# Five conditioning rows moved behind the output evictions, and the first nine rows read their shared row from PSUM

## The reference, cut to what matters

```
# first block, feed-forward
gate, val = split(h @ w_up)            # 1024 -> 2 x 2816
gate = depthwise_conv3(gate)
x = x + g2 * ((silu(gate) * val) @ w_down)     # 2816 -> 1024

# second block, conditioning (six vectors of 1024)
mod = silu(c_2) @ ada_w_2 + ada_b_2    # ada_w_2 is 1024 x 6144
shift1, scale1, gate1, shift2, scale2, gate2 = split(mod)
```

## Time and profile before

| what | value |
|---|---|
| median of 3 runs | 1310.9 us (1310.49 to 1311.98) |
| the profiled execution | 1311.85 us, its span 1310.0 us |
| PE busy | 1259.6 us, 96% of the span |
| DVE, ACT, POOL busy | 822.5, 681.6 and 702.0 us (63, 52 and 54%) |
| mean granted clock of PE | 0.984 |
| chain of work that ended last | PE 77%, DVE 8%, POOL 4%, ACT 4%, DMA 3% |

### The profile page before, as it was taken

One profiled execution on the slowest core, in us unless ns is written; L12 is line 12 of the kernel. 1 busy time (PEld: TensorE's weight loads), 2 busy tenths in 40 slices (PEclk: granted clock), 3 DMA queues, 4 the chain that ended last, 5 costly groups with the idle time before them and its releaser, 6 DMA issues.

```text
span 1310.0 us, 21756 instructions
## 1 busy us (share of the span) xinstructions
PE 1259.6 (96%) x7760; PEld 1070.7 (82%) x7760; DVE 822.5 (63%) x1452; ACT 681.6 (52%) x1273; POOL 702.0 (54%) x582
## 2 busy tenths in 40 slices
PE   8999999999998999999999999999989999999998
PEld 1688888676787799999887788766869999998886
DVE  2577652668537988888886371686267787773113
ACT  3812545685536356666323464587365655653232
POOL 0335153268343957887766824354608666666561
PEclk9999999999998999999999989899999999999999
DMA  9417549032132743223585412110302223233221
GB/s 392 193 49 276 191 161 178 17 115 80 66 116 110 284 167 118 108 96 120 182 327 204 145 65 80 50 50 34 129 1 97 98 99 125 96 103 122 96 96 65
DMA packets 27412, 166.87 MB, mean 127 GB/s; under 512 B 2976, under 2 KB 5280, under 8 KB 8656
## 3 DMA queue, kind: packets, MB, share of 16 engines
q1 hardware_dynamic: 25328, 151.31, 32.6%
q10 hardware_dynamic: 2016, 14.68, 3.0%
HBM read 163.85 MB, written 6.32 MB: 130 GB/s over the span
## 4 chain that ended last, share of the span: by engine, by line
PE 77%; DVE 8%; POOL 4%; ACT 4%; DMA 3%; issue 3%; SPq 0%; DVEq 0%; ACTq 0%; POOLq 0%
PE bank L1641 26%; PE bank L297 21%; PE bank L357 13%; PE bank L333 5%; POOL w_lo L290 2%; DMA ada_ring<-ada_dram 2%; PE bank L1514 1%; DVE ada_ring L2418 1%; PE bank L1486 1%; PE bank L777 1%; PE bank L586 1%; DVE arena L2482 1%; DMA w_raw<-w_dram 1%; PE bank L600 1%; PE bank L572 1%
## 5 line engine op out<-in xcount | busy, mean ns | idle before, releaser
L290 POOL TENSOR_TENSOR w_lo<-w_raw,w_hi 128x512 fp32r<-128x512 f32 x168 | 258.7, 1571 | 331.4 <-ACT w_hi L281 331.4
L297 PE MATMUL bank<-h_hi,w_hi 128*128 128x512 f32 x512 | 205.5, 401 | 8.7 <-DVE h_lo L473 4.1
L1641 PE MATMUL bank<-arena_rounded,w_hi 128*128 128x256 f32 x1152 | 203.2, 278 | 0.0
L297 PE MATMUL bank<-h_lo,w_hi 128*128 128x512 f32 x512 | 202.0, 395 | 0.0
L297 PE MATMUL bank<-h_hi,w_lo 128*128 128x512 f32 x512 | 201.8, 394 | 0.0
L1357 POOL TENSOR_TENSOR w_lo<-w_raw,w_hi 128x512 fp32r<-128x512 f32 x108 | 141.1, 1308 | 102.4 <-ACT w_hi L1869 100.8
L281 ACT ACTIVATE w_hi<-w_raw 128x2048 fp32r<-128x2048 f32 x46 | 88.1, 1916 | 167.4 <-PE bank L357 60.6
L1641 PEld LDWEIGHTS bank<-arena_rounded,w_hi 128*128 128x128 f32 x1152 | 174.9, 188 | 0.0
L1641 PE MATMUL bank<-arena_rounded,w_lo 128*128 128x256 f32 x576 | 159.3, 277 | 0.0
L1641 PE MATMUL bank<-h_hi,w_hi 128*128 128x256 f32 x432 | 122.2, 283 | 1.4 <-DVE arena L2334 1.1
L297 PEld LDWEIGHTS bank<-h_hi,w_hi 128*128 128x128 f32 x512 | 97.9, 191 | 31.4 <-issue 6.7
(11 more groups left out here) (329 smaller groups left out, 2896.7 us busy)
## 6 DMA issues: line engine op xcount, KB each, us to landing
w_raw<-w_dram SPq DMA_DIRECT2D x92, 1024.0 KB, 4.8
ada_ring<-ada_dram SPq DMA_DIRECT2D x30, 1024.0 KB, 5.2
ada_ring<-ada_dram ACTq DMA_DIRECT2D x14, 1024.0 KB, 4.9
arena<-ada_dram SPq DMA_DIRECT2D x4, 1024.0 KB, 9.9
arena<-x_dram SPq DMA_DIRECT2D x2, 2048.0 KB, 11.7
bias_copies<-bias_rows SPq DMA_DIRECT2D x1, 4096.0 KB, 17.7
arena<-bias_copies SPq DMA_DIRECT2D x4, 768.0 KB, 5.8
ada_ring<-rpb_dram SPq DMA_DIRECT2D x16, 128.0 KB, 9.3
```

Of the source, the lines that this page charges most:

```text
L290: last = nc.gpsimd.tensor_tensor(w_lo[b % 2][:, part], w_raw[b % 2][:, part], w_hi[b % 2][:, part], ALU.subtract)
L297: last = nc.tensor.matmul(bank[:, :], w[:, ft, k, :], x[:, k, :], start=k == first and m == 0, stop=k == final and m == 2)
L1641: last = nc.tensor.matmul(product_at[p], w[:, k], x[:, k], start=k == 0 and m == 0, stop=k == 3 and m == 2)
```

## The change

Five edits. Rows 0 to 8 take their second operand from PSUM, as one operand that spans banks 5 and 6 (the eight PSUM tensors become three, at the same places, so that this can be written); DVE waits for PE's `row2_done` there, and for ACT's copy only before the down projection. Rows 19 to 23 leave their places behind splits 9 and 11 and stand one each behind the evictions of f = 0 to 4; the five small operations stand behind the eviction of f = 5. SP's list follows: row 19 behind block 46, 20 behind 47, 21 behind 48, 22 and 23 behind 49. `SQF` moves out of the ring, and ACT's wait for the 48 goes. In the plain blocks POOL takes two of its three extra splits (`low_turned`, 128x1024) one block later.

```diff
-        SQ1, SQ2, SQF = A(A_TMP, 3, 512), A(A_SQ, 3, 512), view(ada, 0, 3, 512)
+        SQ1, SQ2, SQF = A(A_TMP, 3, 512), A(A_SQ, 3, 512), A(A_SQ + 1536, 3, 512)
...
-        DOWN_ROWS = ((9, 10), (11, 12), (13, 14), (15, 16), (17, 18), (19, 20), (21, 22, 23))
+        TURNED_BEHIND = {B_UP + 2: 2, B_UP + 4: 0, B_UP + 5: 3}
+        DOWN_ROWS, LATE_ROWS = ((9, 10), (11, 12), (13, 14), (15, 16), (17, 18)), range(19, 24)
...
             for b in range(B_DOWN + 4, B_QKV + 1):
-                if b < B_DOWN + 10:
+                if b < B_DOWN + 8:
                     load_rows(*DOWN_ROWS[b - B_DOWN - 3])
                 load_block(sp, b)
+                if b >= B_DOWN + 8 and LATE_ROWS[0] + b - B_DOWN - 8 < 24:
+                    load_rows(LATE_ROWS[0] + b - B_DOWN - 8)
+            load_rows(*LATE_ROWS[4:])
             load_block(sp, 50)
...
                 low(pool, b)
-                if b < B_UP + 5:
-                    low_turned(up1, (2, 0, 3)[b - B_UP - 2])
+                if b in TURNED_BEHIND:
+                    low_turned(up1, TURNED_BEHIND[b])
...
-                if f == 0:
-                    act.wait_ge(ada_used, 48)
...
-            dve.wait_ge(row2_out, 2)
+            dve.wait_ge(row2_done, 1)
             row = 0
             for u in range(PLAIN1 - 1):
                 plain_taps(u)
                 for k in range(2 if u else 1):
-                    add_ada2(row)
+                    add_ada2(row, row2_banks)
...
             hidden_low(9, slice(12, 14), 0)
-            rows_behind(5)
             hidden_low(10, slice(16, 18), 2)
             hidden_low(11, slice(14, 16), 0)
-            rows_behind(6)
-            dve.wait_ge(ada_used, 48)
...
             for f in range(DC):
                 dve.wait_ge(half_used, used_after(B_DOWN + 6) + f + 1)
                 nc.vector.scalar_tensor_tensor(out=XR[:, f, :], in0=ps[f][:, :], scalar=modb[:, 24 + f:25 + f], in1=XR[:, f, :],
                                                op0=ALU.mult, op1=ALU.add).then_inc(down_free, 1)
+                if f < len(LATE_ROWS):
+                    add_ada2(LATE_ROWS[f], row2)
+                if f == len(LATE_ROWS):
+                    conditioning()
                 if f < DC - 1:
                     add_squares(dve, 3, f, SQ2)
```

More of the change, by code:

```diff
@@ L128, in sem @@
             return es.enter_context(nc.semaphore(name))
-        ps = [es.enter_context(nc.psum_tensor(f"bank{i}", [P, 512], F32)) for i in range(8)]
+        banks = [es.enter_context(nc.psum_tensor(name, [P, 512 * n], F32)) for name, n in (("bank0to4", 5), ("bank56", 2), ("bank7", 1))]
+        ps = [banks[0][:, 512 * k:512 * k + 512] for k in range(5)] + [banks[1][:, 0:512], banks[1][:, 512:1024], banks[2][:, :]]
+        row2_banks = banks[1][:, :]
         w_raw = [sb(f"w_raw{s}", [P, BLK]) for s in range(2)]
@@ L2420, in add_ada1, with add_ada2 @@
                 last.then_inc(ada_used, 1)
[L2422 to L2428, removed]
-                dve.wait_ge(ada_in[j % 2], 16 * ((24 + j) // 2 - 3))
-                half_dot(j, 0)
-                half_dot(j, 1).then_inc(ada_used, 1)
+            def add_ada2(j, row):
+                dve.wait_ge(ada_in[j % 2], 16 * ((24 + j) // 2 - 3))
+                for f in range(2):
+                    at, src = 2 * j + f, ada[:, j % 2 * BLK + f * D:j % 2 * BLK + (f + 1) * D]
+                    last = nc.vector.tensor_tensor_reduce(out=src, in0=src, in1=row, scale=1.0, scalar=par_("adab2")[:, at:at + 1],
+                                                          op0=ALU.mult, op1=ALU.add, accum_out=mod2[:, at:at + 1])
+                last.then_inc(ada_used, 1)
             def outer_taps(buf, src, w, m, n, done):
@@ L2647, in rows_behind @@
                 for j in DOWN_ROWS[k]:
-                    add_ada2(j)
+                    add_ada2(j, row2)
+            dve.wait_ge(row2_out, 2)
             hidden_low(3, slice(18, 20), 4)
@@ L2655, in _, with conditioning @@
                 rows_behind(1 + t)
+            def conditioning():
+                dve.wait_ge(ada_used, 48)
+                link(nc.vector.scalar_tensor_tensor(out=gain3, in0=mod2[:, 8:16], scalar=1.0, in1=par_("mixpre"), op0=ALU.add, op1=ALU.mult))
+                nc.vector.tensor_tensor(gain3, gain3, par_("final"), ALU.mult)
+                nc.vector.scalar_tensor_tensor(out=gain4, in0=mod2[:, 32:40], scalar=1.0, in1=par_("ffnpre"), op0=ALU.add, op1=ALU.mult)
+                nc.vector.tensor_tensor(post1, mod2[:, 16:24], par_("mixpost"), ALU.mult)
+                nc.vector.tensor_tensor(post2, mod2[:, 40:48], par_("ffnpost"), ALU.mult).then_inc(mod2_ready, 1)
             hidden_low(9, slice(12, 14), 0)
-            rows_behind(5)
             hidden_low(10, slice(16, 18), 2)
             hidden_low(11, slice(14, 16), 0)
-            rows_behind(6)
-            dve.wait_ge(ada_used, 48)
[L2662 to L2666, removed]
             for f in range(DC):
```

## The result

| what | before | after |
|---|---|---|
| median | 1311.4 us (1310.5 to 1314.4, 11 runs) | 1315.4 us (1314.1 to 1320.2, 11 runs) |
| ratio | | 1.0035, 95% interval 1.0026 to 1.0045 |
| span of the profiled execution | 1310.0 us | 1314.4 us |
| mean granted clock there | 0.984 | 0.982 |

By the ratio the changed kernel is 4.6 us slower (3.4 to 5.9; the medians differ by 4.0). The forecast was 1311.2, in a range from 1307.2 to 1314.5; the rival named "slower" had 1315.4. Whether that rival is what happened is a question for the rows, not for the sum.

The account below looks back on a forecast made before the run. PE, hardly ever idle, was taken as the bound, with stops of 4.1 us together (0.3% of the run). Terms -1.7 and +2.0 gave +0.3 on the median 1310.9: 1311.2 us, range 1307.2 to 1314.5.

Parts of the forecast that it names:

- the rival named "slower": Tail before `mean_head`: small operations and last sums each meet a POOL operation, clock down; +4.5 us, 1315.4; chance 0.15.
- part 1: Plain blocks to p5 of block 22: bank operand ends contention with POOL, half rows take 1.27; gain 1.7 us.
- So the gain is kept: Behind p5 of block 22: PE runs on without a stop for 146 us, so the 1.7 us stays won.
- Part 2: Before block 46: with rows 19 to 23 moved, POOL's rest takes 5.1 and PE's 2.0 us stop goes.
- Part 3: First eviction to `mean_head`: DVE and POOL alternate, block 48's rest comes late; loss 2.0 us, block 46's gain already spent.
- I let two of the five meet a POOL operation: Behind eviction 5: two of DVE's five small operations wait for POOL; 1.7 us with their own time.
- The clock: Before `mean_head`: clock falls during PE's new wait, six products slower, about 1.8 us more, 1313.0; chance 0.18.
- not saturated: f = 2 to 7: DVE keeps up, PE never waits; 1307.2, or 1308.8 with block 48's rest late; chance 0.17.
- bank operand without effect: Plain blocks: bank operand goes on contending, only POOL's new split order helps, -0.8 us, 1312.1; chance 0.07.

Follow-up runs that it names:

- part 1 alone: Against the kernel before: rows 0 to 8 read the banks, two POOL splits stand one block later, rows 19 to 23 unmoved; -0.3 us (-2.2 to 1.7).
- the change with block 24 held: Against the changed kernel: SP issues block 24's transfer one POOL operation later; +7.2 us (5.4 to 9.2) to the kernel before.
- the experiment: Against the changed kernel: five small operations moved behind the sum of squares of f = 6; +1.2 us (-0.8 to 3.1) to the kernel before.

## Why the prediction was wrong, point by point

**The bank operand (part 1): right.** The half rows of the plain blocks and POOL's rest beside them, after:

```profile
452.77 1.27 DVE L2431 CUSTOM_DVE_ANT_0 ada_ring<-ada_ring,bank,params 128x1024 f32<-128x1024 f32 x1
...
447.06 5.03 POOL L292 TENSOR_TENSOR w_lo<-w_raw,w_hi 128x512 fp32r<-128x512 f32 x4 [3.47 <-ACT w_hi L283]
```

1.27 and 5.03, where 1.27 and 5.2 were forecast and 2.30 and 7.98 stood before. The stops went: 0.9 in the plain blocks and 0.8 at p5 of block 22, 1.7 as forecast. The surcharge for a PSUM source that the Trainium skill gives (VectorE: DVE Perf Modes, "The TRN2 errata") is not to be seen: a free half row takes 1.27 with either operand.

**"So the gain is kept": the first step that failed.** I had concluded from an unbroken piece of 146 us that there is room behind p5 of block 22. It showed only that PE did not wait when it came 1.8 later. In the old kernel the last share of block 24's transfer is done at 477.8, 0.5 before ACT comes to it, and the taps follow; that cover was not counted. Nor was it that the taps have two SBUF operands and would meet POOL's splits, 3.3 for 1.9. One block later PE waits 0.3 to 2.8 again. The term stood at -1.7 in the sum; it is +1.2 in the profiled execution and -0.3 (-2.2 to 1.7) by the ratio of part 1 alone.

**Part 2, block 46: right.** The stop is gone, -1.9 for -2.0; its rest takes 5.03.

**Part 3, the count of the alternation: right up to f = 5.** Block 46 starts at 715.24 after and was forecast at 714.3 on the old axis, so 0.95 comes off. Row 19 ran from 714.48 to 717.0 (forecast 714.4 to 716.9); block 47's rest was done at 724.0 (723.9), block 48's at 737.7 (737.6); f = 5's eviction began at 742.6 (742.6).

**"I let two of the five meet a POOL operation": the second step that failed, in size.** They took 3.1 us for a forecast 1.7: three of the five met one. From there DVE's list is 1.4 late; the plain sum that I had put ahead of the sum of f = 6 was not in the way (0.69 for 1.4), so `mean_head` begins at 750.35 on the old axis for a forecast 749.6: a loss of 2.8 for 2.0.

**The clock: the third.** I gave its fall before the six products a chance of 0.18 and a price of 1.8. It fell at 751.8, half a us after that wait ended and ahead of the six products; in the other three profiles with this wait it fell 1.1 to 1.6 after it, among the six products. `mean_head`'s lag of 2.8 (750.35 for 747.58) is 5.2 at block 49; the 2.4 between them are the six products, the eight small matmuls of the norm and the first products of block 49 at half clock. The forecast had the stop and the fall as two cases. In the profiles they go together: the stretch at half clock lasts 13.7 to 17.1 us in the four with a wait of 2.8 before `mean_head`, 13.7 in the one with 1.09, and 6.8 to 10.2 in the seven without one. Its price varies: 2.5 behind `mean_head` in three of the four, 0.9 in the change with block 24 held.

Together the three steps come to 1.4 (part 1, by its ratio) + 0.8 + 2.4 = 4.6. With them the forecast of +0.3 becomes +4.9, for a measured +4.6.

**The rival that ended at 1315.4** had the right sum by luck and not the right terms: it kept part 1's gain (-1.7) and had `mean_head` at 752 (by its own words, three more waits of 1.0 behind 749.6, it would be 752.6). What happened is: part 1 about 0, tail +2.8, clock +2.4. The mechanism that it names, small operations in step with POOL, is the one that the experiment shows, at 1.7 of the 2.8. The rivals "not saturated" and "bank operand without effect" are refuted by the rows above.

## What to carry to other kernels

A stretch of an engine without waits says nothing of how much earlier it could run: look at what its suppliers had in hand, and at the transfer with the least slack. When a wait in front of a short tail is forecast, price the tail at the lower clock as part of the same case. And work that shares an access with another engine has a place, not only a quantity: five rows behind the evictions cost 4.6 us and three cost nothing, because only block 48's rest and the last sums before `mean_head` had no time to give.

## What the runs showed of the hardware that I had not expected

- An operation of 8 columns with two SBUF operands, 0.15 long, took 0.59, 1.22 and 1.26 beside POOL in three of five cases (L2660, L2661, L2663). The two longer ones waited 1.07 and 1.11, about the 1.03 for which the prediction has one POOL operation hold the access, whatever their own size. The Trainium skill (GPSIMD Engine Reference, "Key points") names such instructions as contending and says nothing of size; the trace adds that the price is POOL's, not theirs.
- One of the 16 shares of block 24's transfer came 0.9 to 2.6 us behind the others in six of the seven profiles in which a 16 KB fetch of instructions began 0.07 to 0.54 after the issue, and in none of the other five.
- Stretches at half clock come and go in code that is the same: one at 137.6 to 141.0 in the kernel before is missing after and costs PE 1.6 there. A single profile of this kernel is uncertain by that much for each such place, so the comparisons rest on the ratios, and the rows on what is alike in several profiles.
